# Another layout and order of streaming for x, and weight ring slots spaced 32 bytes further apart, in a two-layer hybrid decoder trunk

## The reference, cut to what matters

```python
def swiglu_ffn(h, w_in, w_out):
    gate, up = jnp.split(h @ w_in, 2, axis=-1)
    return (jax.nn.silu(gate) * up) @ w_out
...
h = layer_norm(ALPHA * h + 0.5 * swiglu_ffn(h, w_in, w_out), gain, bias)     # 4 of these, D_FF = 2816
h = layer_norm(ALPHA * h + mixer(h), gain, bias)                             # short_conv, then GLA
```

## Time and profile before

| what | value |
|---|---|
| device time, median of 2 runs | 1007.04 us |
| the profiled execution: its own time | 1007.63 us |
| its span, first to last instruction | 1005.8 us |
| mean granted TensorE clock | 0.998 of full speed |
| TensorE busy | 993.8 us, 99% |
| VectorE busy | 721.1 us, 72% |
| ScalarE busy | 510.8 us, 51% |
| DMA | 176.60 MB, 176 GB/s on average |

### The profile page before, as it was taken

One profiled execution on the slowest core, in us unless ns is written; L12 is line 12 of the kernel. 1 busy time (PEld: TensorE's weight loads), 2 busy tenths in 40 slices (PEclk: granted clock), 3 DMA queues, 4 the chain that ended last, 5 costly groups with the idle time before them and its releaser, 6 DMA issues.

```text
span 1005.8 us, 19130 instructions
## 1 busy us (share of the span) xinstructions
PE 993.8 (99%) x7932; PEld 977.8 (97%) x7932; DVE 721.1 (72%) x1077; ACT 510.8 (51%) x743; POOL 122.6 (12%) x136
## 2 busy tenths in 40 slices
PE   8999999999999999999999999999999999999997
PEld 7999999999999999999999999999989999999986
DVE  5855657689899866557697565667897998866543
ACT  5643445465456543445565444445867766544340
POOL 2000002320002000003220000134152420000000
PEclk9999999999999999999999999999999999999999
DMA  9966656637762866556639665555355747866531
GB/s 249 263 194 181 176 159 179 192 93 209 232 177 81 242 199 181 168 164 183 198 89 259 179 185 156 172 168 161 85 148 145 201 116 234 254 196 197 184 132 42
DMA packets 324264, 176.60 MB, mean 176 GB/s; under 512 B 6658, under 2 KB 320048, under 8 KB 324176
## 3 DMA queue, kind: packets, MB, share of 16 engines
q1 hardware_dynamic: 323664, 174.15, 59.6%
q0 software_dynamic: 480, 1.15, 0.4%
q10 hardware_dynamic: 32, 0.07, 0.0%
HBM read 174.29 MB, written 1.05 MB: 174 GB/s over the span
## 4 chain that ended last, share of the span: by engine, by line
PE 90%; DVE 4%; DMA 1%; ACT 1%; issue 1%; POOL 1%; SPq 0%; POOLq 0%; DVEq 0%; ACTq 0%
PE bank L1318 23%; PE bank L1315 23%; PE bank L1320 23%; PE bank L1334 3%; PE bank L1335 3%; PE bank L1336 3%; PE bank L1475 2%; PE bank L1476 2%; PE bank L1474 2%; PE bank L1359 2%; PE bank L1360 2%; PE bank L1361 2%; DVE weights_lo L823 1%; DMA raw_weights<-in_ffn_w_in_dram 1%; DVE rms L1223 1%
## 5 line engine op out<-in xcount | busy, mean ns | idle before, releaser
L464 ACT ACTIVATE weights_hi<-raw_weights 128x1024 fp32r<-128x1024 f32 x335 | 353.7, 1059 | 403.9 <-PE bank L1320 286.5
L823 DVE TENSOR_TENSOR weights_lo<-raw_weights,weights_hi 128x1024 fp32r<-128x1024 f32 x334 | 417.0, 1255 | 196.0 <-ACT weights_hi L464 194.8
L1315 PE MATMUL bank<-x_hi,weights_hi 128*128 128x272 f32 (+1 forms) x1584 | 225.7, 285 | 0.5 <-ACT consts L628 0.5
L1318 PE MATMUL bank<-x_hi,weights_lo 128*128 128x272 f32 (+1 forms) x1584 | 224.0, 283 | 0.0
L1320 PE MATMUL bank<-x_lo,weights_hi 128*128 128x272 f32 (+1 forms) x1584 | 223.0, 282 | 0.0
L1315 PEld LDWEIGHTS bank<-x_hi,weights_hi 128*128 128x128 f32 x1584 | 206.0, 189 | 1.1 <-ACT consts L628 0.7
L1318 PEld LDWEIGHTS bank<-x_hi,weights_lo 128*128 128x128 f32 x1584 | 204.8, 188 | 0.0
L1320 PEld LDWEIGHTS bank<-x_lo,weights_hi 128*128 128x128 f32 x1584 | 204.2, 187 | 0.0
L1320 PE MATMUL bank<-mid_lo,weights_hi 128*128 128x272 f32 x462 | 67.2, 285 | 0.0
L1318 PE MATMUL bank<-mid_hi,weights_lo 128*128 128x272 f32 x462 | 66.8, 284 | 0.0
L1315 PE MATMUL bank<-mid_hi,weights_hi 128*128 128x272 f32 x462 | 66.7, 284 | 0.0
(11 more groups left out here) (230 smaller groups left out, 1208.6 us busy)
## 6 DMA issues: line engine op xcount, KB each, us to landing
raw_weights<-in_ffn_w_in_dram SPq DMA_DIRECT2D x176, 512.0 KB, 4.6
raw_weights<-in_ffn_w_out_dram SPq DMA_DIRECT2D x70, 512.0 KB, 3.6
raw_weights<-in_conv_w_in_dram SPq DMA_DIRECT2D x24, 512.0 KB, 3.9
raw_weights<-in_gla_w_in_dram SPq DMA_DIRECT2D x24, 512.0 KB, 3.9
raw_weights<-in_ffn_w_out_dram SPq DMA_DIRECT2D x24, 384.0 KB, 3.2
raw_weights<-in_conv_w_out_dram SPq DMA_DIRECT2D x8, 512.0 KB, 4.9
raw_weights<-in_gla_w_out_dram SPq DMA_DIRECT2D x8, 512.0 KB, 5.0
x_tok<-in_x_dram SPq DMA_DIRECT2D x2, 512.0 KB, 4.9
```

Of the source, the lines that this page charges most:

```text
L464: nc.scalar.activation(w_hi[:, n % RING, :], raw[:, n % RAW, :], ACT.Copy).then_inc(hi_split, 1)
L823: nc.vector.tensor_tensor(w_lo[:, s, :], raw[:, n % RAW, :], w_hi[:, s, :].bitcast(F32), ALU.subtract).then_inc(lo_split, 1)
L1315: nc.tensor.matmul(into, block_of(w_hi, n, k - k0), walk(hi[:, k, cols]), start=first and k == k0, stop=False)
L1318: nc.tensor.matmul(into, block_of(w_lo, n, k - k0), walk(hi[:, k, cols]), start=False, stop=False)
```

## The change

x is laid out in two halves: each chunk k has 2 x 160 words, half 0 with the first half of the tokens and half 1, 640 bytes further on, with the rest. Chunks lie 1280 bytes apart for `x_hi` and `x_lo` alike. For 272 tokens a half holds 136, for 256 tokens 128; the close packing is gone. TensorE streams it in the order of `downward`: the last 4 words of half 0, the last 4 words of half 1, the 4 words before them in half 0, and so on down to the start. The PSUM output is addressed in the same order. The rings `w_hi` and `w_lo` get 8 words more per slot, so that slots lie 4128 bytes apart. The 12 tiles of the GLA that took 256 columns now take 272, and what reads their PSUM bank skips the first 16. `pad_y` is gone. Sources other than x (`mid`, `yc`, `y`, `zg`) are streamed as before.

```diff
-        w_hi = sb("weights_hi", [P, RING, KU * P], F32R)
-        w_lo = sb("weights_lo", [P, RING, KU * P], F32R)
-        x_hi_area = sb("x_hi", [P, KD, T + 16], F32R)
-        x_lo_area = sb("x_lo", [P, KD, T + 48], F32R)
-        x_hi, x_lo = x_hi_area[:, :, 0:T], x_lo_area[:, :, 0:T]
...
+        w_hi = sb("weights_hi", [P, RING, KU * P + LINE // 8], F32R)[:, :, 0:KU * P]
+        w_lo = sb("weights_lo", [P, RING, KU * P + LINE // 8], F32R)[:, :, 0:KU * P]
+        x_hi_area = sb("x_hi", [P, KD, 2, HALF_PITCH], F32R)
+        x_lo_area = sb("x_lo", [P, KD, 2, HALF_PITCH], F32R)
...
         def x_of(n_tok):
-            return (x_hi, x_lo, tokens(n_tok)) if n_tok == T else (*x_close, slice(0, SEQ))
+            return x_hi_area[:, :, :, 0:n_tok // 2], x_lo_area[:, :, :, 0:n_tok // 2]
...
+        def in_halves(ap):
+            return ap.rearrange("p (v t) -> p v t", v=2)
...
-                    nc.scalar.activation(out_hi[:, k, out_cols], resid[:, k, cols], ACT.Identity,
+                    nc.scalar.activation(out_hi[:, k, :, :], in_halves(resid[:, k, cols]), ACT.Identity,
...
-                    nc.vector.scalar_tensor_tensor(out=out_lo[:, k, out_cols], in0=resid[:, k, cols], scalar=ln_bias_col(q, k),
-                                                   in1=out_hi[:, k, out_cols].bitcast(F32), op0=ALU.add,
+                    nc.vector.scalar_tensor_tensor(out=out_lo[:, k, :, :], in0=in_halves(resid[:, k, cols]),
+                                                   scalar=ln_bias_col(q, k), in1=out_hi[:, k, :, :].bitcast(F32), op0=ALU.add,
...
+            def downward(halves):
+                return halves.rearrange("p v (l e) -> p l v e", e=4)[:, ::-1, :, :]
+
             def by_rows(ap):
                 return ap.rearrange("p (i j e) -> p j i e", e=4, j=4)
...
-                walk = by_rows if ps.shape[-1] == T else lambda ap: ap
-                into = walk(ps)
+                if len(hi.shape) == 4:
+                    into = downward(in_halves(ps))
+
+                    def streamed(part, k):
+                        return downward(part[:, k, :, :])
+                else:
+                    walk = by_rows if ps.shape[-1] == T else lambda ap: ap
+                    into = walk(ps)
...
-                        nc.tensor.matmul(into, block_of(w_hi, n, k - k0), walk(hi[:, k, cols]), start=first and k == k0, stop=False)
+                        nc.tensor.matmul(into, block_of(w_hi, n, k - k0), streamed(hi, k), start=first and k == k0, stop=False)
...
-                short = HEADS < j <= 2 * HEADS or j > 2 * HEADS + KD
-                cols = main if short else every
-                multiply(bank[tile_bank(j)][:, 0:SEQ if short else T], n0 + j, (x_hi, x_lo), cols,
+                multiply(bank[tile_bank(j)][:, 0:T], n0 + j, (x_hi, x_lo), every,
```

More of the change, by code:

```diff
@@ L78, in hybrid_trunk @@
     LINE = 64
-    CLOSE_AT = 3 * LINE // 4
+    HALF_PITCH = 5 * LINE // 2
+    assert T // 2 <= HALF_PITCH
     ctx = ExitStack()
@@ L501, in normalise @@
                 cols = tokens(n_tok)
-                out_hi, _, out_cols = x_of(n_tok)
+                out_hi, _ = x_of(n_tok)
                 act.wait_ge(stat_ready, 2 * q + 1)
@@ L608, in round_x @@
                 act.wait_ge(x_turned, k + 1)
-                nc.scalar.activation(x_hi[:, k, :], bank[k][:, 0:T], ACT.Copy).then_inc(xhi_ready, 1)
+                nc.scalar.activation(x_hi[:, k, :, :], in_halves(bank[k][:, 0:T]), ACT.Copy).then_inc(xhi_ready, 1)
             def scale_x(k):
@@ L1079, in _ @@
                     nc.vector.tensor_scalar(resid[:, k, :], bank[k][:, 0:T], ALPHA, None, ALU.mult).then_inc(first_resid, 1)
-                nc.vector.tensor_tensor(x_lo[:, k, :], bank[k][:, 0:T], x_hi[:, k, :].bitcast(F32),
+                nc.vector.tensor_tensor(x_lo[:, k, :, :], in_halves(bank[k][:, 0:T]), x_hi[:, k, :, :].bitcast(F32),
                                         ALU.subtract).then_inc(xlo_ready, 1)
@@ L1309, in multiply, with streamed @@
                 hi, lo = source
-                walk = by_rows if ps.shape[-1] == T else lambda ap: ap
-                into = walk(ps)
+                if len(hi.shape) == 4:
[5 more added lines that the diff above has]
+                    into = walk(ps)
+                    def streamed(part, k):
+                        return walk(part[:, k, cols])
                 if ready is None and before_last is None and not middles:
@@ L1314, in multiply @@
                     for k in range(k0, k1):
-                        nc.tensor.matmul(into, block_of(w_hi, n, k - k0), walk(hi[:, k, cols]), start=first and k == k0, stop=False)
+                        nc.tensor.matmul(into, block_of(w_hi, n, k - k0), streamed(hi, k), start=first and k == k0, stop=False)
                     pe.wait_ge(lo_split, n + 1)
                     for k in range(k0, k1):
-                        nc.tensor.matmul(into, block_of(w_lo, n, k - k0), walk(hi[:, k, cols]), start=False, stop=False)
+                        nc.tensor.matmul(into, block_of(w_lo, n, k - k0), streamed(hi, k), start=False, stop=False)
                     for k in range(k0, k1):
-                        mm = nc.tensor.matmul(into, block_of(w_hi, n, k - k0), walk(lo[:, k, cols]), start=False,
+                        mm = nc.tensor.matmul(into, block_of(w_hi, n, k - k0), streamed(lo, k), start=False,
                                               stop=last and k == k1 - 1)
@@ L1333, in multiply @@
                     w_h, w_l = block_of(w_hi, n, k - k0), block_of(w_lo, n, k - k0)
-                    nc.tensor.matmul(into, w_h, walk(hi[:, k, cols]), start=first and k == k0, stop=False)
-                    nc.tensor.matmul(into, w_h, walk(lo[:, k, cols]), start=False, stop=False)
-                    mm = nc.tensor.matmul(into, w_l, walk(hi[:, k, cols]), start=False, stop=last and k == k1 - 1)
+                    nc.tensor.matmul(into, w_h, streamed(hi, k), start=first and k == k0, stop=False)
+                    nc.tensor.matmul(into, w_h, streamed(lo, k), start=False, stop=False)
+                    mm = nc.tensor.matmul(into, w_l, streamed(hi, k), start=False, stop=last and k == k1 - 1)
                 mm.then_inc(unit_used, 1)
@@ L1411, in ffn @@
             def ffn(f, n0, n_tok, q):
-                in_hi, in_lo, cols = x_of(n_tok)
+                x_parts, cols = x_of(n_tok), tokens(n_tok)
                 def tile(t, ready=None):
@@ L1419, in tile @@
                     for half in range(2):
-                        multiply(bank[2 * (t % PAIRS) + half][:, 0:n_tok], n0 + 2 * t + half, (in_hi, in_lo), cols,
+                        multiply(bank[2 * (t % PAIRS) + half][:, 0:n_tok], n0 + 2 * t + half, x_parts, cols,
                                  ready=ready if half == 0 else None)
@@ L1448, in first_multiply @@
                 pe.wait_ge(first_resid, 1)
-                ps = bank[0][:, 0:T]
+                ps = downward(in_halves(bank[0][:, 0:T]))
                 for k in range(KD):
                     pe.wait_ge(xlo_ready, k + 1)
-                    nc.tensor.matmul(ps, block_of(w_hi, n, k), x_hi[:, k, :], start=k == 0, stop=False)
-                    nc.tensor.matmul(ps, block_of(w_hi, n, k), x_lo[:, k, :], start=False, stop=False)
+                    nc.tensor.matmul(ps, block_of(w_hi, n, k), downward(x_hi[:, k, :, :]), start=k == 0, stop=False)
+                    nc.tensor.matmul(ps, block_of(w_hi, n, k), downward(x_lo[:, k, :, :]), start=False, stop=False)
                 pe.wait_ge(lo_split, n + 1)
                 for k in range(KD):
-                    mm = nc.tensor.matmul(ps, block_of(w_lo, n, k), x_hi[:, k, :], start=False, stop=k == KD - 1)
+                    mm = nc.tensor.matmul(ps, block_of(w_lo, n, k), downward(x_hi[:, k, :, :]), start=False, stop=k == KD - 1)
                 mm.then_inc(unit_used, 1)
```

13 lines of the change are left out of this document (4 added, 9 removed).

## The result

The kernel after takes 1042.75 us (median of 2 runs, 1042.67 and 1042.83), the one before 1007.04: a ratio of 1.0344, interval 1.031 to 1.0378. It is slower by 35.7 us. The forecast was 997.4 with a range of 979 to 1017; the time lies outside it.

The account below looks back on a forecast made before the run. The prediction held that only the length of TensorE's row of matmuls sets the time. Terms of -11.4, +0.8 and +1.0 sum to -9.6 us: 998.0 from the profiled run, 997.4 against the median, range 979 to 1017.

Parts of the forecast that it names:

- f3: Stretch of 40 units with close-packed x, 960 matmuls of 256 columns: 114.3 ns each, 1.0 us more in all.
- x with 272 columns: 3672 TensorE matmuls streaming x: 120.0 ns each instead of 123.1, 11.4 us less; bounds 113.3 and 126.6 ns.
- The GLA tiles: 12 tiles, 288 matmuls going from 256 to 272 columns: 120.0 instead of 117.2 ns, 0.8 us more.
- PSUM in pieces: Non-contiguous PSUM output, where it was contiguous before, slows matmuls; 1 ns charged as its price.
- The other sources: `mid`, `yc`, `y`, `zg` and last projection keep their order: 0 change, within 1 ns on some 2800 matmuls, 2.8 us either way.
- in step, but on the wrong foot: Rival: x and weight reads meet at every piece, 131 ns at 272 columns, 43.6 us more, 1051 us; chance 0.13.
- The order does nothing: Rival: matmuls of 272 columns stay at 123.1 ns, leaving only small losses, 1010 us; chance 0.25.
- the steps hold fully: Rival: x and weights never meet, 117 ns for 272 columns, 25.3 us less, 982 us; chance 0.17.

Follow-up runs that it names:

- the best version: Changed kernel with halves 576 bytes apart, chunks 1280, ring slots 4096, x 64 bytes further on and `pad_y` back: 999.31 us, ratio 0.9915 to the kernel before.
- second kernel of streams: 88 matmul streams without the decoder: ten half distances under 32-column loads, 576 and 704 bytes at eight places, both directions; 576 downward, full load: 120.2 ns per matmul.
- third kernel of streams: 94 matmul streams without the decoder, varying chunk steps, column counts and half distances in 16-byte steps; halves 576 apart cost 121.7 ns with chunks 1152, 120.0 with 1280.
- first kernel of streams: 78 streams of 48 matmuls without the decoder, varying x order, PSUM order, half distance, x place and load width; halves 640 apart, 32-column load: 129.0 ns.

## Why the prediction was wrong

**The view of the bottleneck was right.** TensorE's row of matmuls sets the time alone; its clock stays at 2.4 GHz and its waits short; ScalarE's and VectorE's writes of x in two runs cost nothing; the time follows from matmuls times nanoseconds. Even the sum's method was right: in the best version, where 272 columns do cost the 120.0 ns of my sum, and f3 113.3, the sum is -11.4 + 0.8 + 0 = -10.6 us, and 8.0 were measured (1007.3 before, 999.31).

**The step that failed** is *x with 272 columns*: "I take the smallest excess that any long stretch here shows ... 120.0 ns". It measured 129.2 to 130.0, and its upper bound of 126.6, zg's excess, was passed too. 3672 x 9.2 to 10.0 ns are 33.8 to 36.7 us of the 45.4 between forecast and result. I looked at one relation only, x to the weights, because the durations of the earlier trace rows showed the two disturbing each other, and took the walk inside x for free. A stream that alternates between two places has a relation to itself. With halves 640 bytes apart it costs 129.0 ns for 272 columns with the short weight load, and that was in no row before: no source of the kernel before alternates between two places that far apart. The nearest, `by_rows`, moves by 64 bytes at a time and costs 121.0 ns in the streams with the short load. The bound should have been called open at the top.

**f3.** I took 114.3 from the last projection, whose weights are in `by_rows` pieces. Pieces of 16 bytes weren't the point: it measured 121.5. 960 x 7.2 = 6.9 us of the miss. **The GLA tiles** came to 130.3 for the same reason as the rest of x. **PSUM in pieces**, for which I had charged 1 ns, costs nothing in the order of the change (L83, L84).

**The other sources** stayed as predicted: `mid` 284 ns, zg 127.4. **The ring's 32 bytes** I had not priced apart. Alone they cost 7.7 us; within the change no effect is clear of the intervals (1042.75 against 1044.64 without).

**The rivals.** The third, "in step, but on the wrong foot", with 0.13, gave the sign and nearly the size: 131 ns, 124.3 for 256 columns and 1051 us, against 129 to 130, 121.5 and 1042.75. That was luck, for its mechanism was wrong: weight loads all near 195 ns would have shown it, and they stood at 188, and the loss is there with the short load too. Its 11 ns came from the worst matmul of the old order, which has no halves. "The order does nothing" fell, and "the steps hold fully" was never reached: no stretch of 48 matmuls that I read, in streams or kernels, took fewer than 120.0 ns for 272 columns.

**What stays open.** What in SBUF makes the pairs of places good or bad was not found. The data, with the short load: downward, 544 to 576 and 688 to 704 bytes at 120.0 to 120.2 ns, 608 to 672 at 126.5 to 130.2, 768 at 135.4 and 139.6; upward, 576, 640 and 704 between 126.9 and 130.0. 16 bytes decide (576 and 592). Distances that differ by 256 bytes come out alike or nearly so where both were run: 576 and 832 at 120.0 and 120.2, 768 and 1024 at 139.6 and 139.8 in the same kernel, 544 and 800 at 120.0 and 122.1. That fits an effect of the distance modulo 256 bytes, like the chunk steps, but three pairs are all there is. By the Trainium skill, "SBUF — State Buffer", section "Specifications (TRN2)", memory lines are 16 bytes and each crossing to a new line costs; by that alone all these streams, with one line for each piece, would cost the same, and they don't.

## What to carry to other kernels

When a stream alternates between two places, measure the distance and the direction by themselves before building on them: 48 matmuls in a row, with the weight load at a quarter of its width to make the other reader small, take 6 us and tell what 16 bytes are worth. Where a time is matmuls times nanoseconds, an upper bound read from the rows at hand holds only for the address patterns in those rows; a new pattern has no upper bound yet. And an edit of a distance often moves a second one (here the chunks' step): keep the others fixed, or the miss can't be read.

## What the runs showed of the hardware that I had not expected

- The cost of a stream of float32 pieces of 16 bytes, read from two places in turn, runs from 120.0 to 139.8 ns for 272 columns by their distance alone (short load, downward, L85 to L94 of the second kernel of streams), and by 10 ns with the direction.
- At 640 bytes the full weight load adds 0 to 4 ns to that, by the place of x. In the kernel after, where x's own walk is slow, weight loads stay at 188 ns. Where halves are 768 bytes apart they are lengthened too, although that stream is slow with the short load as well (135.4 and 139.6 ns): a long weight load is no proof that x and the weights meet. In the third kernel of streams, line L182:

```profile
L182 PEld LDWEIGHTS bank<-xs,w x48: 188/194/195, 603.7 to 610.2; 128*128 128x128 f32 x48
```

- The least excess over the columns, in the stretches read, is 6.6 to 6.7 ns for 256 and 272 columns. 320 columns, straight, have twice that: 7.04 us / 48 = 146.7 ns where the columns take 133.3, with the full load (L126), and the same with the short one. The walk makes the difference here, not the number: straight through at the same place, 256 columns have 13.5 over too (L123: 120.2), and in halves 1344 bytes apart, downward, 320 columns have 6.9 (L128: 140.2). The timeline of the same kernel:

```profile
243.60 7.20 PE L126 MATMUL bank<-xs,w 128*128 128x320 f32 x48
250.64 7.21 PE L127 MATMUL bank<-xs,w 128*32 128x320 f32 x48
```

- The order of the PSUM output in halves, in pieces of 16 bytes, costs nothing that 48 matmuls show, with the short load or the full one (L134 and L135 of the first kernel of streams: 130.0 and 125.4, against 129.8 and 125.4). In `by_rows` it does show in single streams, either way: with `by_rows` x and the full load 124.8 ns against 120.0 with PSUM straight at one place (L99, L141), and 125.0 against 126.3 at another (L95, L136). Why stays open.
